# Expert products in plain fp32 from 32-token stationaries on four column groups, instead of three fp32r products of high and low parts

## What is computed

```python
def moe_swiglu(x, router, wg, wu, wd):
    xt = x.reshape(b * T, D)                        # D = 1024
    top_v, top_i = lax.top_k(xt @ router, 2)        # 8 experts
    gates = one_hot(top_i) . softmax(top_v)
    for e in range(8):                              # wg, wu: 1024 x 3584, wd: 3584 x 1024
        out = out + swiglu(xt, wg[e], wu[e], wd[e]) * gates[:, e:e + 1]
```

## Time and profile before

| | |
|---|---|
| median of 3 runs | 1637.92 us (1634.76 to 1638.63) |
| span of the profiled execution | 1632.4 us |
| TensorE busy | 1602.5 us, 98% |
| VectorE busy | 1236.8 us, 76% |
| ScalarE busy | 973.7 us, 60% |
| DMA read from HBM | 428.33 MB, 263 GB/s over the span |
| mean granted TensorE clock | 0.986 |

### The profile page before, as it was taken

How to read it: one execution, slowest core, us unless ns; L and a number is a source line. 1 busy time by engine, 2 the same in 40 slices (tenths; PEclk the granted TensorE clock), 3 DMA queues, 4 the chain that set the end, 5 groups by cost and what they waited for, 6 DMA issues and landing times.

```text
span 1632.4 us, 22041 instructions
## 1 busy us (share of the span) xinstructions
PE 1602.5 (98%) x8331; PEld 1337.8 (82%) x8332; DVE 1236.8 (76%) x1174; ACT 973.7 (60%) x882; POOL 75.9 (5%) x88
## 2 busy tenths in 40 slices
PE   8998999999999999999999999999999999999996
PEld 6775699999599587888888888888888888888885
DVE  5488456654656647988898888888888988988983
ACT  3285344432456035776777777777777777777673
POOL 0070000000303300000000000000000000000000
PEclk9999999999999999999999999999999999999998
DMA  9322145566135046998999999999999999999992
GB/s 283 104 88 68 58 160 170 180 197 190 52 112 172 26 155 231 366 374 319 370 373 334 362 368 334 362 370 334 360 370 333 360 378 336 359 370 338 357 371 96
DMA packets 221270, 430.13 MB, mean 263 GB/s; under 512 B 9530, under 2 KB 76608, under 8 KB 220896
## 3 DMA queue, kind: packets, MB, share of 16 engines
q1 hardware_dynamic: 217960, 425.34, 73.0%
q10 hardware_dynamic: 3256, 4.06, 0.8%
HBM read 428.33 MB, written 1.05 MB: 263 GB/s over the span
## 4 chain that ended last, share of the span: by engine, by line
PE 93%; DVE 4%; ACT 1%; DMA 1%; issue 1%; ACTq 0%; DVEq 0%
PE ps L1634 91%; PE ps L1651 2%; DVE arena L1042 1%; DMA raw<-in_moe_w_up_dram 0%; DMA raw<-in_moe_w_gate_dram 0%; DMA arena<-in_meta_tokens_dram 0%; DVE arena L1184 0%; ACT w_hi L928 0%; DVE arena L1127 0%; DVE arena L1125 0%; ACT arena L631 0%; DVE arena L1152 0%; DVE ring_lo L1250 0%; DVE xtk_lo L1433 0%; DVE arena L1153 0%
## 5 line engine op out<-in xcount | busy, mean ns | idle before, releaser
L1414 DVE TENSOR_TENSOR w_lo<-raw,w_hi 128x2048 fp32r<-128x2048 f32 x224 | 511.7, 2291 | 80.9 <-ACT w_hi L928 80.4
L928 ACT ACTIVATE w_hi<-raw 128x2048 fp32r<-128x2048 f32 x224 | 429.1, 1919 | 180.7 <-DMA raw<-in_moe_w_gate_dram 96.6
L1634 PE MATMUL ps<-w_hi,xg_hi 128*128 128x512 f32 x904 | 359.3, 397 | 4.5 <-DVE w_lo L1598 2.1
L1634 PE MATMUL ps<-w_hi,xg_lo 128*128 128x512 f32 x904 | 354.6, 392 | 0.0
L1634 PE MATMUL ps<-w_lo,xg_hi 128*128 128x512 f32 x904 | 354.1, 392 | 0.0
L1418 DVE TENSOR_TENSOR w_lo<-raw,w_hi 128x2048 fp32r<-128x2048 f32 x110 | 251.6, 2288 | 41.2 <-ACT w_hi L932 41.2
L932 ACT ACTIVATE w_hi<-raw 128x2048 fp32r<-128x2048 f32 x110 | 211.1, 1919 | 76.5 <-DMA raw<-in_moe_w_down_dram 75.6
L1634 PEld LDWEIGHTS ps<-w_hi,xg_hi 128*128 128x128 f32 x904 | 170.9, 189 | 39.5 <-DVE w_lo L1598 2.5
L1634 PEld LDWEIGHTS ps<-w_hi,xg_lo 128*128 128x128 f32 x904 | 170.8, 189 | 36.6
L1634 PEld LDWEIGHTS ps<-w_lo,xg_hi 128*128 128x128 f32 x904 | 171.0, 189 | 34.1
L1634 PE MATMUL ps<-w_hi,eh_hi 128*128 128x512 f32 x440 | 173.6, 394 | 3.0 <-issue 3.0
(11 more groups left out here) (298 smaller groups left out, 1874.3 us busy)
## 6 DMA issues: line engine op xcount, KB each, us to landing
raw<-in_moe_w_gate_dram SPq DMA_DIRECT2D x112, 1024.0 KB, 5.1
raw<-in_moe_w_up_dram SPq DMA_DIRECT2D x112, 1024.0 KB, 5.2
raw<-in_moe_w_down_dram SPq DMA_DIRECT2D x112, 1024.0 KB, 5.0
ring<-in_w_in_ab_dram SPq DMA_DIRECT2D x12, 1024.0 KB, 6.5
ring<-in_hy_w_in_dram SPq DMA_DIRECT2D x12, 1024.0 KB, 5.2
ring<-in_ffn_w_gate_dram SPq DMA_DIRECT2D x11, 1024.0 KB, 5.1
ring<-in_ffn_w_up_dram SPq DMA_DIRECT2D x11, 1024.0 KB, 5.2
ring<-in_ffn_w_down_dram SPq DMA_DIRECT2D x8, 1408.0 KB, 6.6
```

Of the source, the lines that this page charges most:

```text
L928: nc.scalar.activation(w_hi[:, j, :], raw[:, j, :], ACT.Copy).then_inc(sem("gu_high"), 1)
L1414: V.tensor_tensor(w_lo[:, j, :], raw[:, j, :], w_hi[:, j, :].bitcast(F32), ALU.subtract).then_inc(sem("gu_split"), 1)
L1634: return nc.tensor.matmul(o, l, r, start=start, stop=stop)
```

## The change

An item has 96 slots instead of 128, as three groups of 32. The gathered rows `xg`, the turned hidden rows `ehT` and the weights stay plain fp32. A 512-column slice is now six plain fp32 matmuls (`columns`): for each token group a 32-column stationary streams the slice's first 384 columns (`MAIN`) into the output partitions of its group, 0 to 95, and the last 128 columns (`SIDE`) of all three groups go, one after another, into partitions 96 to 127. The bank then holds 128 x 384 numbers, and silu, product, transposes (three) and their copy run over that shape.

All splits of weights, gathered rows and hidden rows are gone from ScalarE and VectorE; the token-major rows, `SEL` and the gather are plain fp32 as well. The result is first put together in `ye` (two ScalarE and six VectorE copies), then scaled and split into `ye_hi`, `ye_lo` as before; spreading it back moves from stage 1 to stage 2. The weights go round a ring of 14 places, 12 where `raw`, `w_lo` and `w_hi` were and two in the layer weights' ring slots 2 and 3, in one order for loads and for use. The new functions number an item's 42 units and count them.

Smaller parts: `xw`, `ye` and `ye_hi`, `ye_lo` lie over constant tables that are no longer read; the table of later items allows an expert to have two of them; some semaphores are merged.

```diff
-CAP = 128
+GROUP = 32
+GROUPS = 3
+CAP = GROUP * GROUPS
 WIDE = 512
+SIDE = WIDE // 4
+MAIN = WIDE - SIDE
 STAGES = FEXP // WIDE
+UNITS = 14
+PER_ITEM = 6 * STAGES
+ABSENT = (0, 1, 6, 7)
...
-        with ExitStack() as early:
-            raw = early.enter_context(nc.sbuf_tensor("raw", [P, 6, 2048], F32))
-        w_lo = sb("w_lo", [P, 6, 2048], F32R)
-        w_hi = sb("w_hi", [P, 6, 2048], F32R)
-        xg_hi = sb("xg_hi", [P, KT, CAP], F32R)
-        xg_lo = sb("xg_lo", [P, KT, CAP], F32R)
-        eh_hi = sb("eh_hi", [P, 4, CAP], F32R)
-        eh_lo = sb("eh_lo", [P, 4, CAP], F32R)
-        xtk_hi = sb("xtk_hi", [P, 2, D], F32R)
-        xtk_lo = sb("xtk_lo", [P, 2, D], F32R)
-        ye_hi = sb("ye_hi", [P, D], F32R)
-        ye_lo = sb("ye_lo", [P, D], F32R)
-        esg = sb("esg", [P, WIDE])
-        eh = sb("eh", [P, WIDE])
-        SEL = sb("SEL", [P, 2, CAP], F32R)
+        raw = overlay("raw", 0, 12, 2048, dt=F32)
+        raw_ring = overlay("raw_ring", arena_n + 2 * SLOT, 2, SLOT, dt=F32)
+        sb("held", [P, 12 * 2048])
+        unit = [raw[:, r, :] for r in range(12)] + [raw_ring[:, r, 0:2048] for r in range(2)]
+        xg = sb("xg", [P, KT, CAP])
+        esg = sb("esg", [P, MAIN])
+        eh = sb("eh", [P, MAIN])
+        ehT = sb("ehT", [P, GROUPS, P])
...
+        def gate_up_at(s, j):
+
+            return 2 + 6 * s + j
+
+        def down_at(s, j):
+
+            return 6 + 6 * s + j
+
+        def consumed(i, p):
+
+            if isinstance(i, int) and i == 0:
+                return p + 1 - sum(q < p for q in ABSENT)
+            return PER_ITEM * i + (p + 1 - len(ABSENT))
+
+        def unit_in(p):
+
+            return sem(f"unit_in{p % UNITS}")
+
+        def arrivals(i, p):
+
+            return 16 * (PER_ITEM // UNITS) * i + 16 * (p // UNITS + 1 - (p % UNITS in ABSENT))
...
+            def free(i, p):
+
+                if isinstance(i, int) and i == 0:
+                    if p < UNITS or p - UNITS in ABSENT:
+                        return
+                    sp.wait_ge(sem("unit_used"), consumed(0, p - UNITS))
+                else:
+                    sp.wait_ge(sem("unit_used"), PER_ITEM * i + (p - UNITS + 1 - len(ABSENT)))
...
+                for s in range(STAGES):
                     for j in range(4):
-                        load_gu(j, STAGES * i + s, e, s, True)
-                    for j in range(2):
-                        if s > 1 or not first:
-                            load_d(j, STAGES * i + (s - 1), e, s - 1, s > 1 or not first)
+                        load_gu(i, s, j, e)
+                    if s == 0 and not first:
+                        for j in range(2):
+                            load_d(i, down_at(0, j), STAGES - 1, j, before)
+                    if first and s == 1:
+                        for n in (1, 3):
+                            sp.wait_ge(sem("tile_ready"), NUMBER[("ho", n)] + 1)
+                    if 0 < s < STAGES - 1:
+                        for j in range(2):
+                            load_d(i, down_at(s, j), s - 1, j, e)
...
-            def high_gu(j, S):
-                act.wait_ge(sem(f"unit_in{j}"), 16 * S + 16)
-                nc.scalar.activation(w_hi[:, j, :], raw[:, j, :], ACT.Copy).then_inc(sem("gu_high"), 1)
...
-            def silu(S):
-                act.wait_ge(sem("gu_used"), 4 * S + 2)
-                nc.scalar.activation(esg[:], bank[0][:, :], ACT.Silu).then_inc(sem("sg_ready"), 1)
-
-            def turned_high(S):
+            def silu(i, s):
+                S = STAGES * i + s
+                act.wait_ge(sem("unit_used"), consumed(i, gate_up_at(s, 1)))
+                if s or not isinstance(i, int):
+                    act.wait_ge(sem("h_ready"), S)
+                nc.scalar.activation(esg[:], bank[0][:, 0:MAIN], ACT.Silu).then_inc(sem("sg_ready"), 1)
+
+            def turned_hidden(i, p, S):
+
                 act.wait_ge(sem("turned"), S + 1)
-                nc.scalar.activation(eh_hi[:].rearrange("p a b -> p (a b)"), bank[2][:, :], ACT.Copy).then_inc(sem("eh_high"), 1)
-
-            def gathered_high(i):
+                if p is not None:
+                    act.wait_ge(sem("unit_used"), consumed(i, p))
+                nc.scalar.activation(ehT[:].rearrange("p a b -> p (a b)"), bank[2][:, 0:MAIN], ACT.Copy).then_inc(sem("ehT_ready"), 1)
+
+            def gathered(i):
+                act.wait_ge(sem("gather_ready"), 2 * i + 1)
+                nc.scalar.activation(xg[:, 0:4, :].rearrange("p a b -> p (a b)"), bank[6][:, 0:4 * CAP], ACT.Copy).then_inc(sem("xg_first"), 1)
...
+            def result(i, p):
+
+                act.wait_ge(sem("unit_used"), consumed(i, p))
                 for half in range(2):
-                    act.wait_ge(sem("gather_ready"), 2 * i + half + 1)
-                    nc.scalar.activation(xg_hi[:, 4 * half:4 * half + 4, :].rearrange("p a b -> p (a b)"), bank[6 + half][:, :],
-                                         ACT.Copy).then_inc(sem("xg_high"), 1)
-
-            def result_high(n):
-
-                act.wait_ge(sem("d_used"), 2 * STAGES * n)
+                    nc.scalar.activation(ye[0:CAP, 512 * half:512 * half + MAIN], bank[4 + half][0:CAP, 0:MAIN], ACT.Copy).then_inc(sem("ye_main"), 1)
+                act.wait_ge(sem("selt_ready"), 2 * i)
                 for half in range(2):
                     c = slice(512 * half, 512 * half + 512)
-                    nc.scalar.activation(ye_hi[:, c], bank[4 + half][:, :], ACT.Identity, scale=gslot[:, 0:1]).then_inc(sem("ye_high"), 1)
+                    act.wait_ge(sem("ye_main"), 2 * i + (half - 1))
+                    act.wait_ge(sem("ye_side"), 6 * i + (3 * half - 3))
+                    nc.scalar.activation(ye_hi[0:CAP, c], ye[0:CAP, c], ACT.Identity, scale=gslot[0:CAP, 0:1]).then_inc(sem("ye_high"), 1)
...
-            def low_gu(j, S):
-                dve.wait_ge(sem("gu_high"), 4 * S + (j + 1))
-                V.tensor_tensor(w_lo[:, j, :], raw[:, j, :], w_hi[:, j, :].bitcast(F32), ALU.subtract).then_inc(sem("gu_split"), 1)
...
+                V.tensor_tensor(eh[:], esg[:], bank[1][:, 0:MAIN], ALU.mult).then_inc(sem("h_ready"), 1)
...
+                V.tensor_copy(xg[:, 4:8, :].rearrange("p a b -> p (a b)"), bank[7][:, 0:4 * CAP]).then_inc(sem("xg_second"), 1)
...
+                        V.tensor_copy(ye[GROUP * g:GROUP * g + GROUP, 512 * half + MAIN:512 * half + WIDE],
+                                      bank[4 + half][CAP:P, SIDE * g:SIDE * g + SIDE]).then_inc(sem("ye_side"), 1)
...
-            def gate_up(j, S):
-
-                pe.wait_ge(sem("gu_split"), 4 * S + (j + 1))
-                w = [a[:, j, :].rearrange("p (k n) -> p k n", k=4) for a in (w_hi, w_lo)]
+            def columns(o, rows, w, start, stop):
+
+                for g in range(GROUPS):
+                    mm(o[GROUP * g:GROUP * g + GROUP, 0:MAIN], rows[g], w[:, 0:MAIN], start, stop)
+                for g in range(GROUPS):
+                    last = mm(o[CAP:P, SIDE * g:SIDE * g + SIDE], rows[g], w[:, MAIN:WIDE], start and g == 0, stop and g == GROUPS - 1)
+                return last
+
+            def gate_up(i, s, j):
+
+                p = gate_up_at(s, j)
+                if s or not isinstance(i, int):
+                    if j == 0:
+                        pe.wait_ge(sem("sg_ready"), STAGES * i + s)
+                    if j == 2:
+                        pe.wait_ge(sem("h_ready"), STAGES * i + s)
+                pe.wait_ge(unit_in(p), arrivals(i, p))
+                w = unit[p % UNITS].rearrange("p (k n) -> p k n", k=4)
                 for k in range(4):
                     kk = 4 * (j % 2) + k
-                    last = product(bank[j // 2][:, :], xg_hi[:, kk, :], xg_lo[:, kk, :], [a[:, k, :] for a in w], kk == 0, kk == KT - 1)
-                last.then_inc(sem("gu_used"), 1)
-
-            def turn_hidden(S):
+                    rows = [xg[:, kk, GROUP * g:GROUP * g + GROUP] for g in range(GROUPS)]
+                    last = columns(bank[j // 2], rows, w[:, k, :], kk == 0, kk == KT - 1)
+                last.then_inc(sem("unit_used"), 1)
+            def turn_hidden(S, first=False):
                 pe.wait_ge(sem("h_ready"), S + 1)
-                for j in range(4):
-                    last = turn(bank[2][:, P * j:P * j + P], eh[:, P * j:P * j + P])
+                if not first:
+                    pe.wait_ge(sem("ehT_ready"), S)
+                for c in range(GROUPS):
+                    last = turn(bank[2][:, P * c:P * c + P], eh[:, P * c:P * c + P])
                 last.then_inc(sem("turned"), 1)
...
+            def down(i, at, S, begin=False, end=False, units=(0, 1)):
+
+                pe.wait_ge(sem("ehT_ready"), S + 1)
                 for j in units:
-                    pe.wait_ge(sem("d_split"), 2 * S + (j + 1))
-                    w = [a[:, at + j, :].rearrange("p (k n) -> p k n", k=2) for a in (w_hi, w_lo)]
+                    p = at + j
```

(54 more changed lines are left out.)

230 lines of the change are left out of this document (88 added, 142 removed).

## The result

The changed kernel takes 1659.03 us (median of 4 runs, 1655.91 to 1661.05) where the kernel before takes 1636.34 us beside it: ratio 1.0142, 95% interval 1.0121 to 1.0163.

What follows compares the result with a forecast made beforehand. TensorE was taken to bound the expert part, transfers some 10% behind. Gains of 36.4 (product), 6.2 (transposes), 3.5 (start) and 4 (end) less 23 (shape changes) gave 27.1 us less: 1611 us, 8 in 10 between 1597 and 1730.

Steps and rivals of the forecast that it cites:

- End: Behind the last item: loop exit's 2.98 us stays, wait for the last down unit's low part goes; 4 us gained.
- issue-bound rival: Gate, up and down products: TensorE's sequencer cannot keep a pass each 55 ns; 1698 or about 1730 us; chance 0.16.
- range of 8 in 10: Whole kernel's time: 1597 us (645 ns slices) to 1730 us (issue-bound, a slice of 744 ns).
- Granted clock 1.0 throughout: Expert part, an expected sign: TensorE's granted clock stays at 1.0 throughout.
- The product, 655 ns: Expert products: four column groups side by side, a 512-column slice takes 655 ns instead of 682; 36.4 us gained.
- Changing shape, 0.27 us: Transposes, gathers, tables, result additions: 86 round trips of array shape at 0.27 us; 23 us lost, 17 to 26.
- Start, 3.5 us: Before and in the first stages: split waits and half the slow clock's cost go; 3.5 us gained, 2 to 6.
- Transfers: Expert weight loads: 111 us an item against TensorE's 121.5 (363 GB/s); DMA would be late next.
- The sum: Whole kernel: all gains less the shape changes' loss make 27.1 us less, 1611 us.
- the 5.5 us between span and median: Whole kernel: 1637.9 us median against 1632.4 us profiled span, taken as time around the span and added to 1605.3.
- In-order completion: Expert products: narrow passes may not end before wide ones issued ahead; slice 1080 or 1190 ns, 2180 us; chance 0.08.
- Small losses: Expert part: slices at 670 to 680 ns and shape switches at 0.30 us; 1631 to 1645 us; chance 0.12.

Runs made afterwards that it cites:

- the first experiment: The changed kernel with TensorE's eight items written out one after another instead of a loop over seven: 1606.95 us, ratio 0.9821.
- the last experiment: The written-out changed kernel with table transposes, result additions and next gather set behind a stage's transposes, 29 shape changes fewer: 1597.79 us, ratio 0.9773.

## Why the prediction was wrong

**The step that failed** is in "End": "The loop's exit costs 2.98 us of issue; it stays." I read the one jump whose cost show and took it for a constant of the kernel. I did not ask why the other six jumps of the same loop cost nothing in the trace of before, nor what the change does to that reason. It makes the body some three and a half times as long; the count of instructions stood in my own issue-bound rival, but only as a rate. The missing term is six jumps at 5.1 us and the low clock behind each, 3 us: about 49 us. With it the sum would have been 27 - 49, slower by 22 us; measured, 23. The first experiment, which takes the jumps out and wins 52 us, shows that this term is the one that was missing. The exit too got dearer: the chain has 3.53 and 1.55 us of issue there, and a clock of 0.60 from 1624 to 1632. That 1659 us lies inside the range of 8 in 10 (1597 to 1730) is luck: the range reached that far for the issue-bound case, which did not happen.

**"Granted clock 1.0 throughout"** was wrong for that reason alone: from item to item it fell only at and behind stops, and in the written-out kernel it is 1.00 from 640 to 1560 us.

**The product, 655 ns.** Right. Twelve slices more in a piece take 15.86 - 8.00 = 7.86 us, 655 ns each. A stage of 24 slices takes 16.34 us (forecast 16.3), an item without jump 121.55 (121 to 122). The four groups of unequal length run side by side for whole items, not only in a burst.

**Changing shape, 0.27 us.** Right in size, a little low: 0.32 us by the last experiment, against 0.27 and a range of 0.20 to 0.30. For 86 that is 27.5 us instead of 23, just past the range's 26.

**Start, 3.5 us.** Mis-sized: the first stage's transposes end at 631.32 us instead of 637.70, 6.4 earlier, with the gathers starting together (613.8 and 613.9). Two windows of TensorE in the kernel before, beside the one in the earlier trace rows:

```profile
616.00:620.00 4.00, 2.43 (x17) 0.83 0.00 0
...
624.00:628.00 4.00, 4.00 (x16) 0.82 0.50 151
```

In the changed kernel the clock is 1.00 in all of them. I had counted half of the 2 us that the window at 0.50 costs. By an estimate from these clocks all of it went, and so did 0.7 us in each neighbour (4 us at 0.83 and 0.82): 3.4 instead of 1. With the waits (1.6 and 0.9) that is 5.9, and the shorter stage (16.34 for 16.81) brings the rest.

**End, 4 us.** In the written-out kernel the time from the last item's gather to the end of the span is 152.2 us for 157.5. An item's own gain is 2.4 of these 5.3 us, so 2.9 are the end's, instead of 4. In the changed kernel the same time is 157.4 us: the clock behind the sixth stop (2.0), the longer stops at the exit and the low clock there ate the gain.

**Transfers.** Right: no load holds TensorE in the expert part, whose DMA rate is 366 GB/s written out (forecast 363). What is late next was not DMA but code, on the same DMA engines.

**The sum.** 27 us less were forecast, and the first experiment shows 28. So the sum was right for a kernel without the jump back, but in part by luck: the start brought 2.4 us more than its 3.5, the end 1.1 less than its 4, and the changes of shape cost up to 4.5 more than their 23. One reading in it is wrong without moving the forecast: the 5.5 us between span and median do not lie around the span. For the changed kernel's profiled execution that is 1655.91 - 1654.1 = 1.8 us; the rest is most likely how far the profiled execution of before lay below its median.

**The rivals.** Issue-bound: refuted, since 55 ns a pass stood for whole items and 37 ns for 8 us at a time. The Trainium skill (TensorE: Matmul & The Clock Gate, "Wait — 56ns, not 53.3ns?" in Part 1) states about 62 ns per MATMUL with hardware decode off; that case isn't this kernel's, whose passes come every 55 ns. In-order completion: refuted, the slice would be 1080 ns. The strict reading of Part 3 of that page of the Trainium skill, matmuls that start and end strictly in program order, falls with it. Small losses around 680 ns: refuted, the slice is 655. None of them was what made the kernel slower; what did, a new wait at the loop's jump, was not on my list.

## What to carry to other kernels

When a change multiplies the instructions of an engine inside a hardware loop, look whether the loop's code was being fetched again before, on the instruction queue, and price each jump back: here nothing for a body that stayed (some 1,200 records), and for one that didn't 5 us and 3 of low clock (some 4,200), or 2 us and 3.5 to 5 of low clock (some 2,400 with longer matmuls). Write the loop out on that engine, or cut the number of jumps; covering with filler work here traded one loss for another. And a rate that code sustains in a burst says nothing about the rate at which its instructions arrive.

## What the runs showed of the hardware

- A loop body of some 1,200 TensorE records was not fetched again in the six passes after its first; bodies of some 2,400 and some 4,200 were, with a stop at every jump back (kernel before, body doubled, changed kernel). The length at which it begins was not measured.
- A jump back to code that is no longer there stopped TensorE for 4.3 to 5.5 us with 351 to 401 GB/s of loads during the stop, and for 2.8 to 3.8 us at 154 to 207 GB/s; straight-line code at one 16 KB block per 7 us cost nothing, at one per 5 us (one run) it stopped several times an item.
- With matmuls of 227 ns queued at the jump, 2 us of the stop were left.
- Plain fp32 matmuls on four column groups, three of 384 columns beside three of 128 in turn, run at 655 ns a slice for whole items; changing to full-width 128-column work and back costs 0.32 us.
- After a stop of 4.3 to 5.5 us TensorE ran in part at 1.2 GHz (granted clock 0.53 over 6.4 us behind the third), which cost 1.8 to 4.6 us each time. Stops of 2 us behind 227-ns matmuls cost 3.5 and 5.1 us of it; with zeros ahead of the jump, stops of 1 to 3 us did so after three jumps of six.
